# Decoder trunk on one core: the MLP up projections turned round to stationary activations, with 32x32 block transposes and moves inside SBUF

## What is computed

```python
def _conv_ffn(h, w_up, conv_w, conv_b, w_down):
    u = h @ w_up
    S = u.shape[1]
    up = jnp.pad(u, ((0, 0), (CONV_WIDTH - 1, 0), (0, 0)))
    c = conv_b
    for j in range(CONV_WIDTH):
        c = c + up[:, j:j + S] * conv_w[j]
    gate, val = jnp.split(c, 2, axis=-1)
    return (jax.nn.silu(gate) * val) @ w_down
```

## Time and profile before

| | |
|---|---|
| median of the runs | 2215.7 us |
| the profiled execution | 2215.34 us, span 2213.6 us |
| PE busy | 2208.1 us, 100% of the span |
| PE weight loads busy | 1931.8 us, 87% |
| DVE busy | 1483.8 us, 67% |
| ACT busy | 1176.9 us, 53% |
| POOL busy | 15.1 us, 1% |
| granted TensorE clock | full in every slice (2.4 GHz) |
| the 16 DMA engines | 406.70 MB on SP's queue, 55.9% of their time |

### The profile page before, as it was taken

The page is one execution under the profiler, slowest core; times in us unless marked ns, Lnnn a source line. Parts: engine busy times, 40 slices in busy tenths (PEclk is TensorE's granted clock), DMA queues, the critical chain, the costliest instruction groups (busy, mean ns, idle before and its releaser), DMA issues.

```text
span 2213.6 us, 34732 instructions
## 1 busy us (share of the span) xinstructions
PE 2208.1 (100%) x12450; PEld 1931.8 (87%) x12450; DVE 1483.8 (67%) x1753; ACT 1176.9 (53%) x1409; POOL 15.1 (1%) x21
## 2 busy tenths in 40 slices
PE   9999999999999999999999999999999999999999
PEld 8888898888888888888899888888888888888887
DVE  7666556677777777555578888667777777774443
ACT  7565555555555555444455466555555555553333
POOL 0000000000000000000020000000000000000000
PEclk9999999999999999999999999999999999999999
DMA  7455545555555555555566544455555555566664
GB/s 271 166 169 176 171 162 181 200 181 192 187 197 182 191 188 192 189 190 190 191 212 198 177 158 138 160 183 197 179 199 180 198 181 198 181 196 201 200 198 137
DMA packets 113828, 411.54 MB, mean 186 GB/s; under 512 B 12768, under 2 KB 13536, under 8 KB 113760
## 3 DMA queue, kind: packets, MB, share of 16 engines
q1 hardware_dynamic: 112320, 406.70, 55.9%
q10 hardware_dynamic: 1008, 2.30, 0.3%
q0 software_dynamic: 432, 1.57, 0.2%
HBM read 408.42 MB, written 2.10 MB: 185 GB/s over the span
## 4 chain that ended last, share of the span: by engine, by line
PE 99%; DMA 0%; SPq 0%; DVE 0%; ACT 0%; issue 0%; DVEq 0%
PE psum L1303 99%; DMA raw<-w_all 0%; PE psum L1618 0%; PE psum L1554 0%; DVE w_lo L748 0%; ACT w_hi L289 0%; SPq L237 0%; SPq L235 0%; DVE upad L824 0%; SPq L236 0%; SPq L234 0%; DVEq L83 0%
## 5 line engine op out<-in xcount | busy, mean ns | idle before, releaser
L748 DVE TENSOR_TENSOR w_lo<-raw,w_hi 128x1024 fp32r<-128x1024 f32 x769 | 934.9, 1223 | 676.1 <-ACT w_hi L289 670.1
L1303 PE MATMUL psum<-xg,w_hi 128*128 128x512 f32 (+1 forms) x3936 | 1359.0, 392 | 0.8 <-DVE xg L759 0.6
L289 ACT CAST w_hi<-raw 128x1024 fp32r<-128x1024 f32 x770 | 802.9, 1049 | 768.5 <-PE psum L1303 765.8
L1303 PE MATMUL psum<-xg,w_lo 128*128 128x256 f32 (+1 forms) x3920 | 1089.3, 278 | 0.0
L1303 PEld LDWEIGHTS psum<-xg,w_hi 128*128 128x128 f32 x3936 | 735.7, 187 | 156.6 <-issue 3.0
L1303 PEld LDWEIGHTS psum<-xg,w_lo 128*128 128x128 f32 x3920 | 741.1, 189 | 2.8 <-issue 2.2
L1303 PE MATMUL psum<-hid,w_hi 128*128 128x512 f32 x704 | 244.1, 391 | 0.0
L1303 PE MATMUL psum<-w_hi,hid 128*128 128x512 f32 x704 | 217.7, 390 | 0.0
L1303 PE MATMUL psum<-hid,w_lo 128*128 128x256 f32 x704 | 197.1, 280 | 0.0
L1303 PE MATMUL psum<-att,w_hi 128*128 128x512 f32 x512 | 178.8, 393 | 0.0
L1303 PEld LDWEIGHTS psum<-hid,w_hi 128*128 128x128 f32 x704 | 131.6, 187 | 28.9
(11 more groups left out here) (174 smaller groups left out, 1059.5 us busy)
## 6 DMA issues: line engine op xcount, KB each, us to landing
raw<-w_all SPq DMA_DIRECT2D x770, 512.0 KB, 3.7
xres<-x_in SPq DMA_DIRECT2D x3, 512.0 KB, 8.9
cst<-consts_in ACTq DMA_DIRECT2D x2, 768.0 KB, 5.8
raw<-w_all SPq DMA_DIRECT2D x2, 256.0 KB, 3.5
xres<-x_in SPq DMA_DIRECT2D x2, 256.0 KB, 4.3
out_t<-part POOLq DMA_DIRECT2D x1, 512.0 KB, 6.9
out_t<-conv POOLq DMA_DIRECT2D x1, 512.0 KB, 7.3
out_t<-gates POOLq DMA_DIRECT2D x1, 512.0 KB, 7.3
```

The lines of the kernel that those rows point to most:

```text
L289: act.copy(w_hi[:, c % RING, :], raw[:, c % RING, :]).then_inc(hi_ready, 1)
L748: dve.tensor_tensor(w_lo[:, c % RING, :], raw[:, c % RING, :], f32(w_hi[:, c % RING, :]), ALU.subtract).then_inc(lo_ready, 1)
L1303: return pe.matmul(o, lhsT, rhs, start=start, stop=True, skip_group_check=True)
```

## The change

Both up projections now use `proj_tokens`: the activations are stationary and the weights stream past them. A piece is then 12 matmuls of 512 columns instead of 8 of 512 and 8 of 256 (6,144 columns either way), with 12 weight loads instead of 16. The result has tokens on partitions: two PSUM banks (one for each half of the tokens) by 512 channels. To give the convolution its layout back:

- ACT scales each bank in place by the norm's scale, now one number per partition (2 instructions per half, in place of the copy).
- DVE turns each bank in 32x32 blocks into `turned`, which is the memory of `part` (2 instructions, in place of the add and the multiplication).
- POOL issues four transfers per half, 176 in all, that move `turned` to `upad`, each from 32 partitions to 128, 128 KB in runs of 256 bytes (512 runs).
- The later slots move: first tap from 8 and 16 to 10 and 18, where ACT now waits for the transfers (`up_moved`); other taps from 9 and 17 to 11 and 19; silu from 10 to 13; the product from 18 to 20; `hid` from 19 and 20 to 21 and 22.
- PE waits for the transposes (`up_turned`) before it uses a bank again.

The host orders the up weights' columns for this, and the two norms in front of the MLPs store even and odd tokens apart (`halves`, `by_token`). For these norms only two columns of statistics are computed, not 256. SP's loop over pieces is written in other pieces, with the same transfers in the same order.

```diff
@@ gpsimd
+            def move_up(layer, i, val):
+                u = 2 * UPG * layer + 2 * i + val
+                pool.wait_ge(up_turned, 2 * u + 2)
+                for b in range(4):
+                    pool.dma_start(upad[:, :, 2 + 64 * b:2 + 64 * b + 64],
+                                   turned[32 * b:32 * b + 32, :, :, :].rearrange("i (q c) j h -> i q c (j h)", q=4)).then_inc(up_moved, 16)
...
@@ scalar
                 if e in (7, 15):
                     act.wait_ge(piece_used, base + 16 * i + e + 1)
-                    act.copy(part[:, :, :], psum[:, 4 * val:4 * val + 4, T:2 * T]).then_inc(ub_copied, 1)
-                if e in (8, 16):
-                    act.wait_ge(up_scaled, u + 1)
+                    if e == 7:
+                        act.wait_ge(rs_ready, 2 * layer + 2)
+                    for th in range(2):
+                        act.activation(psum[:, 4 * val + th, :], psum[:, 4 * val + th, :], ACT.Copy, scale=rs[:, T + th:T + th + 1]).then_inc(up_copied, 1)
+                if e in (10, 18):
+                    act.wait_ge(up_moved, 64 * u + 64)
...
-                if e == 10:
+                if e == 13:
                     act.wait_ge(tap2, u + 1)
...
-                if e == 19:
+                if e == 21:
                     act.wait_ge(gated, f + 1)
...
@@ vector
                 if e in (7, 15):
-                    dve.wait_ge(ub_copied, u + 1)
-                    dve.tensor_tensor(part[:, :, :], psum[:, 4 * val:4 * val + 4, 0:T], part[:, :, :], ALU.add).then_inc(acc_free, 1)
-                    dve.wait_ge(acc_free, GROUPS * layer + 4 + 2 * i + val + 1)
-                    dve.tensor_tensor(upad[:, :, 2:T + 2], part[:, :, :], over_heads(rs[:, 0:T], 4), ALU.mult).then_inc(up_scaled, 1)
-                if e in (9, 17):
+                    for th in range(2):
+                        dve.wait_ge(up_copied, 2 * u + th + 1)
+                        dve.transpose(turned[:, :, :, th], psum[:, 4 * val + th, :].rearrange("p (c j) -> p c j", j=32)).then_inc(up_turned, 1)
+                if e in (11, 19):
                     dve.wait_ge(tap0, u + 1)
...
@@ tensor
-                    proj(base + e, fi, 16, 4 * (e // 8), xg, 2, 2 * (e % 8), 512, e % 8 == 0)
+                    bank = 4 * (e // 8)
+                    proj_tokens(base + e, fi, 16, ((psum[:, bank, :], True), (psum[:, bank + 1, :], True)), 2, 2 * (e % 8), 512, e % 8 == 0)
```

More of the change, by code:

```diff
@@ L65 @@
 NPIECES = BASE_WO[1] + WO + UP + DN
-GROUPS = 4 + 2 * UPG + 4
+GROUPS = 8
 V_GAIN = 0
@@ L227, in times, with by_token, halves @@
             return 0 if i is None else i * n
+        turned = part[:, :, :].rearrange("p k t -> p (k t)").rearrange("p (c j h) -> p c j h", h=2, j=32)
+        def by_token(ap):
+            return ap.rearrange("p (j h) -> p j h", h=2)
+        def halves(ap):
+            return ap.rearrange("p (h j) -> p j h", h=2)
         block = ctx.enter_context(nc.Block())
@@ L243, in _, with piece, pieces @@
             sp_q.dma_start(avg_d[:, :], consts_in[:, NC:NC + P]).then_inc(avg_in, 16)
[L244 to L251, removed]
+            def piece(c, i=None, per=0):
+                sp_q.wait_ge(lo_ready, times(i, per) + c - RING + 1)
+                sp_q.dma_start(raw[:, c % RING, :], wg[:, bass.ds(times(i, per) + c, 1), :]).then_inc(raw_full[c % RING], 16)
+            def pieces(first, end):
+                loops = (end - first) // RING
+                with sp_q.Fori(0, loops) as i:
+                    for c in range(first, first + RING):
+                        piece(c, i, RING)
+                for c in range(first + RING * loops, end):
+                    piece(c)
+            sent = RING
+            for layer in range(2):
+                ahead = BASE_WO[layer] + WO + 2 * RING
+                pieces(sent, ahead + 7)
+                with sp_q.Fori(0, UPG) as i:
+                    for e in range(7, 23):
+                        piece(ahead + e, i, 16)
+                sent = ahead + 7 + UP
+            pieces(sent, NPIECES)
             for n in (0, 2):
@@ L272, in _ @@
             pool.memset(ones[:, :], 1.0).then_inc(tables_ready, 1)
+            for i in range(UPG):
+                for val in range(2):
+                    move_up(1, i, val)
             for g in range(3):
@@ L297, in norm @@
                 for k in range(4):
-                    act.activation(xg[:, 4 * g + k, 0:T], xres[:, 4 * g + k, :], ACT.Copy, scale=gain(m, 4 * g + k)).then_inc(xhi_ready, 1)
+                    x_hi, x_in_ = xg[:, 4 * g + k, 0:T], xres[:, 4 * g + k, :]
+                    if m % 2:
+                        x_hi, x_in_ = halves(x_hi), by_token(x_in_)
+                    act.activation(x_hi, x_in_, ACT.Copy, scale=gain(m, 4 * g + k)).then_inc(xhi_ready, 1)
                 if m:
@@ L791, in recip @@
                 dve.wait_ge(root_ready, m + 1)
-                n = T if m % 2 else T + 2
-                dve.reciprocal(rs[:, 0:n], rs[:, 0:n]).then_inc(rs_ready, 1)
+                n = T if m % 2 else 0
+                dve.reciprocal(rs[:, n:T + 2], rs[:, n:T + 2]).then_inc(rs_ready, 1)
             def add_group(o, g, bank0):
@@ L1373, in stat @@
                     pe.wait_ge(avg_in, 16)
-                last = mm(psum[:, bank, 0:T], avg_d[:, :], gates[:, 0, :], True)
-                if m % 2 == 0:
+                if m % 2:
+                    for th in range(2):
+                        last = mm(psum[:, bank, T + th:T + th + 1], gates[:, 2, th * P:(th + 1) * P], avg_d[:, 0:1], th == 0)
+                else:
+                    mm(psum[:, bank, 0:T], avg_d[:, :], gates[:, 0, :], True)
                     for th in range(2):
@@ L1519, in up_body @@
                 for e in range(16):
-                    if e % 8 == 0:
-                        pe.wait_ge(acc_free, GROUPS * layer + 3 + 2 * i + e // 8)
+                    if e % 8 == 0 and m is not None:
+                        pe.wait_ge(acc_free, GROUPS * layer + 3 + e // 8)
+                    if e % 8 == 0 and m is None:
+                        pe.wait_ge(up_turned, 4 * UPG * layer + 4 * i - 2 + e // 4)
                     if m is not None and e < 8 and e % 2 == 0:
@@ L1539, in mlp_layer @@
                 if layer == 0:
-                    out_groups(base + UP, layer, FT // 2, hid, 4 + 2 * UPG,
+                    out_groups(base + UP, layer, FT // 2, hid, 4,
                                lambda e: hid_ready(layer, e))
@@ L1754, in mlp @@
     def mlp(layer):
-        up = a["up"][layer]
+        up = a["up"][layer].reshape(D, 2 * UPG, 4, 32, 4).transpose(0, 1, 4, 2, 3).reshape(D, 2 * FF)
         both = np.concatenate([_pieces(up[:, :FF], 2, 512), _pieces(up[:, FF:], 2, 512)], axis=1)
```

37 lines of the change are left out of this document (22 added, 15 removed).

## The result

The changed kernel takes **2307.1 us** (median of 2304.73 and 2309.49), against 2215.7 before: a ratio of 1.041, with a 95% interval from 1.039 to 1.044. It is slower by 91 us. The forecast was 2197 us, with a range up to 2280. L, the time from the end of the second transpose to the landing of the fourth transfer, is 8.8 us in the median, not 6.3. The time lies beside the second rival's example (2307 at L = 9).

A forecast was written before the change was run, and what follows sets the result against it. PE's matmul issue was taken to bound the kernel. Span 2213.6 - 18.8 - 0.1 + 0 (L = 6.3 hidden) = 2194.7 us, plus 1.7 around it and 0.4 for the median: 2197 us, range 2193 to 2280.

The forecast's parts named there:

- the second rival's example: Transfers to `upad` landing late with L = 9: 2197 + 44 x 2.5 = 2307 us; its rival had chance 0.22.
- The gain at PE: Up projections: 0.053 us less for each of 352 pieces, 18.8 us in all.
- The rule for the loop: Up-projection loop: 30.5 + 2L must fit 43.5 us per iteration; beyond, 44 us lost per us of L.
- the two chains: Work from a half's transfer landing to the next second transpose: 17.1 us from the second half, 13.4 from the first.
- the limit: Largest L hidden in the up-projection loop: 6.5 us, or 5.5 if a transpose costs 1.22.
- Between: 1.0 us an issue ... and 3.3 for the last: POOL's four transfers per half: three issues of 1.0 us plus a last landing of 3.3, so L = 6.3 us.
- the bounds of L: POOL's transfers per half: L from 4.4 us to 11.7, the upper using POOL's 512 KB landing of 7.3 us.
- The second one: Rival: moves to `upad` land late, making the kernel over 2% slower, from L = 7.95; chance 0.22.
- Its first way: POOL's transfers of 512 runs: 1.46 us an issue with 4 us for the last, L = 8.4.
- Its second way: DMA engines in the up stages: full if a run costs over 71 ns, so weights come late too.
- The third: Rival: POOL writes descriptors only while DVE idles, four issues taking 15 us, L about 17, 2659 us; chance 0.04.
- The fourth rival: No gain at PE: the loop holds triples at 0.693 us, not 0.68, giving 2216 us; chance 0.01.

The follow-up runs named there:

- the kernel with late slots and one added matmul: Changed kernel with first taps moved to slots 14 and 22, later work after them, plus one 1-column matmul before layer 0's down projection: 2196.8 us, ratio 0.992.
- The run with one transfer: Changed kernel with only the first of each half's four transfers, 512 runs, 128 KB: 2202.0 us.
- the kernels whose transfers are covered: Changed kernel without transfers (2201.4 us), with a quarter of the runs (2203.0), one transfer (2202.0), SP issuing (2202.2), or first taps at slots 14 and 22 (2201.5).
- with 128 runs: Changed kernel with four transfers kept per half, each moving one of its four channel groups, 32 KB: 2203.0 us, ratio 0.995.
- that with eight transfers: Changed kernel with eight transfers of 256 runs per half in place of four of 512, same bytes: 2402.6 us, ratio 1.085.

## Why the prediction was wrong

**What held.** The gain at PE was forecast at 18.8 us, and the kernel with late slots and one added matmul is 18.7 us under the 2215.5 that the kernel before took on the same chip. The transposes take 0.69 us (0.68 taken) and the scalings 0.65 (0.58 taken). The rule for the loop held almost to the digit: the two chains were summed to 17.1 and 13.4 us and measure 17.07 and 13.66, and the price of 44 us for each us of L measured 43.6. By the measured chains the limit would be 6.4 us. No kernel had a median L between 5.7 (free) and 8.8, so the limit itself wasn't tried from close by. One remark didn't hold: that a change under 2% can hardly be told from none. The interval of 0.990 to 0.993 for the best kernel leaves no doubt of its gain.

**The step that failed is the size of L**, in "Between: 1.0 us an issue ... and 3.3 for the last". The issue was 0.75, the start of the first 0.3 us behind the transposes (put at nothing), and the last landing 6.2. I sized it by a transfer of ACT's on a queue of its own, when the row of POOL's own transfers, 7.3 us, was in hand and used only as the far end. And I added one lone landing to three issues, as if four transfers that follow each other did not get in each other's way. The run with one transfer shows that 3.3 is right for one alone; the three ahead of it add 1.7 us each, not 0.75. The sum of the parts: with the median L, 44 x (8.77 - 6.5) = 100 us, less 18.8, is +81; with the mean, which has POOL's pauses in it, 44 x (9.01 - 6.5) = 110, less 18.8, is +92, and +91 was measured. The pauses I had not seen coming: five of them, four inside a half's transfers, with L 10.1 to 11.9 us there.

**The range failed with it.** Its upper end was L = 8.4, set by a chance of 0.19 for all that lay above, though the bounds of L reached 11.7. With the limit at 6.5 in the middle of what L could be, and a slope of 2% for each us, the upper end should have been 2350 (L = 10) or more.

**Rivals.** The second one has the outcome right, moves that land late, but not the reason. Its first way was issues of 1.46 us and 4 for the last; they were 0.75 and 6.2, and that its example of L = 9 hit the mean L is luck. Its second way, full engines, fell with 16 ns a run. The third, POOL held by DVE, is refuted by the half shown above: POOL issued from 565.62 to 568.59 while DVE ran three conversions on end, and took 0.749 us an issue:

```profile
565.25 3.45 DVE L789 TENSOR_TENSOR w_lo<-raw,w_hi 128x1024 fp32r<-128x1024 f32 x3
```

That agrees with what the Trainium skill (SBUF — State Buffer, Who interferes with whom) lets one expect of tensor-tensor operations. The Trainium skill's two-term price of a GpSimd transfer (DMA: Bandwidth & Descriptors, Anatomy of one DMA), an estimate of 2.3 us for 128 KB, fits no row here: 3.3 alone in the median (2.8 at least), 6.1 for the fourth of four. The fourth rival is out; triples run at 0.680 in the loop. What no rival named is the pace of the stage behind it, worth 4.5 us in the kernels whose transfers are covered; the changed kernel had the fast pace and owes none of its loss to it.

## What to carry to other kernels

In a hand-ordered loop add up the chain from a landing round to the next issue: the slack of a late transfer is the loop's time less that sum, and past it every us is paid in each turn (43.5 less 30.7 here, to be shared by the two L of an iteration). When a new transfer's latency decides, size it by the rows of the same issuing engine and with the transfers ahead of it, and when the forecast hangs on that one number, let the range span its bounds. A wait placed just ahead of the work that feeds the next transfer (slots 14 and 22 here) makes a slow transfer free without making it faster.

## What the hardware showed besides

- **Transfers issued by GpSimd in a row landed late here.** One of 512 runs of 256 bytes lands in 3.3 us, four in a row make the last land 6.2 us after its issue, at 0.75 us an issue (0.61 with 256 runs, 0.54 with 128).
- **GpSimd pauses 3 to 6 us after some 15,000 runs.** In the changed kernel after each 31 transfers, as here:

```profile
587.92 2.23 POOL L290 DMA_DIRECT2D upad<-part  x3 [19.33 <-DVE part L1052]
596.25 0.76 POOL L290 DMA_DIRECT2D upad<-part  x1 [6.10 <-issue]
```

  with 256 runs after each 60 transfers, and with 128 runs once, 3.2 us, after 113. Runs alone don't agree (15,872, 15,360 and 14,464). With 16 further entries for each transfer (16 to 22 would do) they agree: 16,368, 16,320 and 16,272 entries, and one transfer more would be 16,896, 16,592 and 16,416. So a store of something between 16,368 and 16,416 entries that runs full would explain all three; that there is one is inferred, not seen.
- **The pace of a stream of matmuls can depend on the few that stand ahead of it.** Pairs of 512 and 256 columns ran a whole stage at 0.347 or 0.353 us. An added matmul of 1 or of 128 columns changed the pace, two changed it back. It isn't a matter of odd and even in PE's records, where one added matmul is two and two are four; and nothing shows what inside PE it is, nor why a standstill had the same effect as one matmul.
- **The clock fell where PE waited.** The changed kernel's granted clock is 0.995 in the mean, that with eight transfers 0.976, the others 1.0. At the entry of layer 0's down projection PE stood still for 2.65 and 1.83 us. Behind that the changed kernel's first pairs are 0.64 us apart, nearly twice 0.347, at a granted clock of 0.50 (the level of 1.2 GHz), and from 931 us on they are at full pace. PE's timeline, and a stretch with the granted clock ahead of the DMA share:

```profile
922.52 0.50 PE L1347 MATMUL psum<-w_hi,xg 128*128 128x512 f32 x1 [2.65 <-DVE w_lo L789]
...
927.36 0.60 PE L1347 MATMUL psum<-hid,w_hi 128*128 128x512 f32 x1 [1.83 <-DVE w_lo L789]
...
928.61 0.63 PE L1347 MATMUL psum<-hid,w_hi 128*128 128x512 f32 x1
...
929.25 0.63 PE L1347 MATMUL psum<-hid,w_hi 128*128 128x512 f32 x1
...
928.00:929.00 1.00, 1.00 (x4) 0.85 (x4) 1.00 (x2) 1.00 (x2) 0.00 (x0) 0.50 0.62 115
```
